# First feed-forward block by seven block products instead of eight, with its inner activations and the residual kept in DRAM

## What is computed

```python
x = x + y                                     # y = delta rule output @ w_out ("dn_out")
x = x + squared_relu_mlp(rms_norm(x, norm_mlp), mlp_w_up, mlp_w_down)
...
def squared_relu_mlp(h, w_up, w_down):        # 1024 -> 4096 -> 1024
    return jnp.square(jax.nn.relu(h @ w_up)) @ w_down
...
x = rms_norm(x, norm_final)                   # end of the first block
mx = split(silu(c) @ w_mod + b_mod, 6)        # modulation of the second block: needs no x
hx = rms_norm(x, g_norm1) * (1 + mx[1]) + mx[0]
```

## Time and profile before

| | |
|---|---|
| median of 3 runs | 3104.36 us (3101.61 to 3105.61) |
| profiled execution, its time | 3103.91 us |
| its span, first to last instruction | 3102.1 us |
| TensorE busy | 2953.6 us (95% of the span) |
| VectorE, ScalarE, GpSimd busy | 59%, 39%, 29% |
| mean granted TensorE clock | 0.987 |

### The profile page before, as it was taken

How to read it: one execution, slowest core, us unless ns; L and a number is a source line. 1 busy time by engine, 2 the same in 40 slices (tenths; PEclk the granted TensorE clock), 3 DMA queues, 4 the chain that set the end, 5 groups by cost and what they waited for, 6 DMA issues and landing times.

```text
span 3102.1 us, 37785 instructions
## 1 busy us (share of the span) xinstructions
PE 2953.6 (95%) x14715; PEld 2445.9 (79%) x14715; DVE 1820.8 (59%) x2359; ACT 1210.9 (39%) x1929; POOL 901.7 (29%) x684
## 2 busy tenths in 40 slices
PE   7899999989999999999998999999989999999997
PEld 6688888878788888888876777888878778887886
DVE  7566566564365544333366886554574866666866
ACT  5555555553311112221334776222332444444222
POOL 5333332221000000000302886331331444443423
PEclk9999999999999999999999999999999999999999
DMA  3111111112143333111210001011023144446953
GB/s 128 41 48 48 48 48 48 42 62 102 41 129 110 111 113 102 48 48 54 93 53 21 11 9 49 28 35 35 21 75 149 40 157 150 148 148 239 371 207 122
DMA packets 96833, 274.00 MB, mean 88 GB/s; under 512 B 9232, under 2 KB 31248, under 8 KB 92176
## 3 DMA queue, kind: packets, MB, share of 16 engines
q1 hardware_dynamic: 96656, 271.58, 25.0%
HBM read 208.43 MB, written 60.36 MB: 87 GB/s over the span
## 4 chain that ended last, share of the span: by engine, by line
PE 81%; DVE 10%; ACT 4%; issue 3%; POOL 1%; DMA 1%; SPq 0%; POOLq 0%; DVEq 0%; ACTq 0%
PE ps L663 25%; PE ps L1756 11%; PE ps L3068 11%; PE ps L3729 9%; PE ps L3096 7%; DVE b L3677 2%; PE ps L2659 2%; PE ps L1060 1%; DVE b L652 1%; PE ps L2466 1%; PE ps L2437 1%; PE ps L2465 1%; PE ps L1067 1%; PE ps L2480 1%; PE ps L90 1%
## 5 line engine op out<-in xcount | busy, mean ns | idle before, releaser
L663 PE MATMUL ps<-b 128*128 128x512 f32 x3912 | 1009.6, 403 | 29.7 <-DVE b L652 14.4
L663 PEld LDWEIGHTS ps<-b 128*128 128x128 f32 x3912 | 711.4, 191 | 159.2 <-issue 20.1
L1756 PE MATMUL ps<-b 128*128 128x512 f32 x1536 | 361.7, 396 | 0.6 <-DVE b L1924 0.6
L1756 PEld LDWEIGHTS ps<-b 128*128 128x128 f32 x1536 | 288.0, 188 | 69.5 <-DVE b L1924 1.0
L3729 PE MATMUL ps<-b 128*128 128x512 f32 (+1 forms) x1464 | 326.1, 377 | 6.3 <-ACT b L3788 5.9
L3729 PEld LDWEIGHTS ps<-b 128*128 128x128 f32 x1464 | 253.8, 191 | 55.6 <-issue 10.6
L644 ACT ACTIVATE b<-b 128x1024 fp32r<-128x1024 f32 x138 | 145.2, 1054 | 319.5 <-PE ps L1756 242.3
L3121 ACT ACTIVATE b<-b 128x512 fp32r<-128x512 f32 x232 | 142.3, 615 | 270.9 <-PE ps L3096 106.3
L652 DVE TENSOR_TENSOR b<-b 128x1024 fp32r<-128x1024 f32 x138 | 174.2, 1264 | 107.6 <-ACT b L644 98.5
L3068 PE MATMUL ps<-b 128*128 128x512 f32 x960 | 225.9, 393 | 6.0 <-DVE b L3371 3.8
L3068 PEld LDWEIGHTS ps<-b 128*128 128x128 f32 x960 | 180.5, 189 | 48.3 <-DVE b L3371 7.7
(11 more groups left out here) (372 smaller groups left out, 5011.4 us busy)
## 6 DMA issues: line engine op xcount, KB each, us to landing
inner<-b SPq DMA_DIRECT2D x77, 512.0 KB, 2.6
b<-inner SPq DMA_DIRECT2D x35, 1024.0 KB, 13.5
b<-in_down SPq DMA_DIRECT2D x52, 512.0 KB, 4.3
b<-in_mod SPq DMA_DIRECT2D x96, 256.0 KB, 2.6
b<-scratch SPq DMA_DIRECT2D x46, 512.0 KB, 4.4
b<-in_gu SPq DMA_DIRECT2D x44, 512.0 KB, 4.1
b<-in_dn_in SPq DMA_DIRECT2D x32, 512.0 KB, 4.9
b<-in_up SPq DMA_DIRECT2D x32, 512.0 KB, 3.7
```

What stands on the lines that cost most here:

```text
L663: ins = e.matmul(ps[:, c], w, h[:, k, c], start=first and k == 0 and i == 0, stop=last and k == KT - 1 and i == 2)
L1756: ins = e.matmul(ps[:, c], w, u[:, at[k], c], start=k == 0 and p == 0, stop=k == n - 1 and p == 2)
```

## The change

- The feed-forward block of the first layer goes by class `WideSquare`. The inner width of 4096 is 16 tiles v of 256. The first (v = 0) is computed plainly, by 96 matmuls; v = 1 to 15 and the 16 tiles of the down projection take 7 products of 12 matmuls each. A product is a step s, with (v, i) its tile and its number.
- In the up part every tile gives seven pieces (in the second layer it takes two tiles for seven), which go to a DRAM tensor and come back for the down part. x is stored to DRAM after the first residual sum, and read back in the down part; the output is summed in another tile, w.x.
- The norm's factor is not applied to the hidden activations but, squared, to the output: in the last tile (`dve_square_last`) VectorE multiplies each of 16 half rows of the output by it and then adds x, one waiting for the other.
- The modulation's generators are advanced in `pe_project`, twice per unit from the third on, and then at steps 6 to 94 that are multiples of 3, and later on even steps of the down part (`beside`).
- ScalarE starts the two squares per k of the second block's norm (`act_stat2`, now line 1612) when `x1` of k = 3 is complete, since the tiles that they are written to hold the output of k = 0 to 3 until then. GpSimd's 12 sums stay as they are.

Places in the order, and the generators' turns:

```diff
+BLOCKS1 = tuple(((2 * b, 2 * b + 1),) for b in range(8))
+PIECES7 = (0, 3, 5, 4, 1, 2, 6)
...
+    def piece(self, s):
+
+        n = self.na
+        for p in range(n):
+            if p < n - 2:
+                m = s - self.index[p, self.last(p)] - 2
+            else:
+                m, odd = divmod(s - self.index[n, 0] - 14 * (p - n + 2), 2)
+                m = -1 if odd else m
+            if 0 <= m < 7:
+                return p, m
+        return None
...
+    def sums(self, s):
+
+        if s == self.index[self.na, 0] + 13:
+            return self.na - 1
+        if s == self.index[0, 3] + 4:
+            return 0
+        v = self.which(s - 1, "last")
+        return v if v is not None and 0 < v < self.na - 1 else None
...
+    def beside(self, s):
+
+        a, b = self.index[self.na - 2, 0], self.index[self.na, 0]
+        return 6 <= s < a and s % 3 == 0 or s >= b and s % 2 == 0
...
+                if beside and k in (2, 5):
+                    next(beside)
```

SyncE's and TensorE's programs in the products:

```diff
+            piece = w.piece(s)
+            if piece:
+                p, n = piece
+                e.wait_ge(*V.at("tlo", p, n))
+                e.dma_start(self.scratch[4][PIECES7[n], :, p, :],
+                            w.stage[(7 * p + n) % 3].bitcast(F32)).then_inc(*self.hst[(7 * p + n) % 3].up(w.name, p, PIECES7[n]))
...
+            if (v, i) == (w.na + 6, 0):
+                for m in range(7 * w.na - 3, 7 * w.na):
+                    e.wait_ge(*self.hst[m % 3].at(w.name, m // 7, PIECES7[m % 7]))
+                for k in range(KT):
+                    e.wait_ge(*self.xl[k].at("x1_stored"))
+                    e.dma_start(self.x1[:, k, :], self.scratch[2][:, k, :]).then_inc(*self.xl[k].up("x1"))
...
+                if i == 2:
+                    e.wait_ge(*A.at("s1", v))
+                if i == 3:
+                    e.wait_ge(*A.at("s5", v))
+                if i == 4:
+                    e.wait_ge(*A.at("s2", v))
...
+                if i == 5 and v > 3:
+                    e.wait_ge(*V.at("q11", v - 2))
+                if i == 6:
+                    e.wait_ge(*V.at("q22", v))
```

ScalarE's:

```diff
+        for s in range(4, len(w.steps)):
+            v, i = w.steps[s]
+            t = v - w.na
+            if v < w.na:
+                u = w.quads(v)
+                if i in (0, 1, 2, 6):
+                    e.wait_ge(*P.at("st", v, i))
+                if i < 3:
...
+                    e.activation(u[name], self.square_bank(v, i % 2), ACT.Copy).then_inc(*A.up(("s1", "s5", "s2")[i], v))
+                if i == 6:
+                    if v >= 2:
+                        e.wait_ge(*V.at("tlo", v - 2, PIECES7.index(5)))
+                        e.wait_ge(*G.at("t", v - 2, 6))
+                    square(v, "21", self.square_bank(v, 0))
...
+            self.act_wide_high(e, w, s + 6)
+            if v < w.na and 3 <= i < 6:
+                name = ("12", "22", "11")[i - 3]
+                e.wait_ge(*V.at("q" + name, v))
+                square(v, name)
...
+                p, n = piece
+                m = 7 * p + n
+                product = PIECES7[n]
+                if m >= 3:
+                    e.wait_ge(*self.hst[m % 3].at(w.name, (m - 3) // 7, PIECES7[(m - 3) % 7]))
...
+                if product in (0, 3, 5):
+                    e.wait_ge(*A.at("sq", p, {0: "11", 3: "22", 5: "21"}[product]))
+                else:
+                    e.wait_ge(*G.at("t", p, product))
+                e.activation(w.stage[m % 3][:, 0:512], w.source(p, product), ACT.Copy).then_inc(*A.up("thi", p, n))
+            if v == last:
+                for k in {2: (0, 1), 3: (2, 3)}.get(i, ()):
+                    e.wait_ge(*V.at("x1", k))
+                    if k == 0:
+                        e.wait_ge(*V.at("x1", 3))
+                        e.wait_ge(*A.at("cw"))
+                    self.act_stat2(e, self.m1, w.sig, k)
...
+        for _ in beside:
+            pass
+        for k in range(4, KT):
+            e.wait_ge(*V.at("x1", k))
+            self.act_stat2(e, self.m1, w.sig, k)
+        self.act_weights(e, w.j0 + 2)
```

VectorE's:

```diff
+            if v < w.na:
+                if 3 <= i < 6:
+                    name = ("12", "22", "11")[i - 3]
+                    u = w.quads(v)[name]
+                    e.wait_ge(*P.at("st", v, i))
+                    if i == 3:
+                        e.wait_ge(*A.at("s2", v))
+                    e.tensor_tensor(u, u, self.square_bank(v, (1, 0, 2)[i - 3]), ALU.add).then_inc(*V.up("q" + name, v))
+            else:
+                self.dve_square_add(e, w, v - w.na, i)
+            self.dve_wide_low(e, w, s + 6)
+            piece = w.piece(s)
+            if piece:
+                p, n = piece
+                b = w.stage[(7 * p + n) % 3]
+                e.wait_ge(*A.at("thi", p, n))
+                e.tensor_tensor(b[:, 512:1024], w.source(p, PIECES7[n]), b[:, 0:512].bitcast(F32),
+                                ALU.subtract).then_inc(*V.up("tlo", p, n))
+            if v == last:
+                for k, f in {0: ((0, 0), (0, 1)), 1: ((1, 0), (1, 1)), 2: ((2, 0), (2, 1)), 3: ((3, 0), (3, 1), (4, 1), (6, 1)),
+                             4: ((5, 1), (7, 1)), 5: ((4, 0), (6, 0)), 6: ((5, 0), (7, 0))}[i]:
+                    self.dve_square_last(e, w, k, f)
...
+    def dve_square_last(self, e, w, k, f):
+
+        P, A, V, G = w.sig
+        c = HALVES[f]
+        y, x = w.x[:, k, c], self.x1[:, k, c]
+        e.wait_ge(*P.at("rw"))
+        e.wait_ge(*V.last())
+        e.tensor_tensor(y, y, self.psl[3][:, c], ALU.mult).then_inc(*V.up("scaled", k, f))
+        e.wait_ge(*self.xl[k].at("x1"))
+        e.wait_ge(*V.last())
+        ins = e.tensor_tensor(x, x, y, ALU.add)
+        ins.then_inc(*V.up("x1", k) if (f == 1) == (k < 4) else V.up("x1", k, "half"))
```

GpSimd's:

```diff
+            self.pool_wide_sums(e, w, s, 1)
+            p = w.sums(s)
+            if p is not None:
+                u, tq = w.quads(p), w.tq
+                if p:
+                    e.wait_ge(*V.at("tlo", p - 1, 6))
...
+                e.tensor_tensor(tq[0], u["12"], u["11"], ALU.subtract).then_inc(*G.up("t", p, 1))
+                e.wait_ge(*G.last())
+                e.tensor_tensor(u["12"], u["22"], u["12"], ALU.subtract).then_inc(*G.up("t", p, 4))
+                e.tensor_tensor(tq[1], u["22"], tq[0], ALU.subtract).then_inc(*G.up("t", p, 2))
+                e.wait_ge(*G.last())
+                e.tensor_tensor(tq[2], u["21"], tq[1], ALU.subtract).then_inc(*G.up("t", p, 6))
```

917 lines of the change are left out of this document (461 added, 456 removed).

## The result

The changed kernel takes 3163.7 us (median of 4 runs, 3162.3 to 3167.9), the kernel before 3103.8 us: ratio 1.0196, interval 1.0178 to 1.0213, 60 us slower. The forecast was 3107, the range up to 3134. The profiled execution's span is 3166.1 us, 64.0 more than before.

The account below looks back on a forecast made before the run. The prediction took TensorE's matmuls to bound the block. Its terms, -84.9 + 35 + 44 + 6 + 3 = +3 us on a span of 3102.1, gave a forecast of 3107 us, with an 8-in-10 range of 3072 to 3134.

Parts of the forecast that it names:

- What is removed, 84.9 us: First layer's feed-forward block: fewer product matmuls take TensorE from 706.7 to 621.8 us, -84.9 us.
- What is added at the end, +35: Last tile to next layer: GpSimd's sums start only after x1 of k = 3, +35 us with clock, bounds 25 and 40.
- What is added in the up part, +44: Twelve up-part rounds: a dependent chain of 21.5 us against TensorE's 20, plus pairs and clock, +44 us, bounds 5 and 70.
- By sums of busy time the others fit: Up-part round of 20.0 us on TensorE: ScalarE busy 15 us, GpSimd 10, VectorE 14, so each fits.
- the pairs: Up part: the modulation's VectorE instruction pairs delay the chain, 18 to 36 us over twelve rounds, taken as 22.
- the loop through the t sums: Up part: piece splitting, GpSimd's four t sums, S2 and q22 wait for each other in a 21.5 us chain per round.
- Smaller terms, entry +6: Block entry: late VectorE, waits for differences and squares, and two-column tiles, less old gap and clock: +6 us, bounds -4 and 16.
- Smaller terms, down part +3: Down part: 1 MB loads and stores as in the second layer, where TensorE stayed full: +3 us, bounds 0 and 8.
- Up-part traffic, 0: Up part: pieces, weights and modulation move about 290 GB/s, below the 379, so no cost.
- the chain is worse: Rival, 20%: up part, every pair meets GpSimd between q12 and q22, rounds of 25 us, up part 70, 3133 us.
- The full lock: Rival, 3%: VectorE and GpSimd exclude each other for whole instructions, 0.27 us more per meeting, 23 us in all, 3130 us.
- The marks named ahead: Signs: TensorE idle over 20 us at the end; up-part waits for 2009 and 3564; four t sums 6 us or more.

Follow-up runs that it names:

- e5: Changed kernel without the modulation's steps 3 to 9 of twelve (loads, VectorE instructions, small matmuls), so work is left out: 3123.4 us.
- e13: Changed kernel, with TensorE taking the modulation's small matmuls one pair later from its fifth step on and VectorE's accumulators alternating: 3162.2 us.
- e1: Changed kernel, with GpSimd's first three t sums waiting for earlier pieces and the fourth placed behind S2 and S4: 3159.7 us.
- e9: Changed kernel, with the four t sums of every tile made by VectorE instead of GpSimd: 3156.4 us.
- e6: Changed kernel without GpSimd's four t sums of tiles 1 to 15, so work is left out: 3129.6 us.
- e8: Changed kernel, with four buffers instead of two for the modulation's weights up to its tenth step: 3162.9 us.
- e14: Changed kernel, with the twelve operand differences at the block's entry made by VectorE instead of GpSimd: 3158.5 us.
- e7: Changed kernel, with the modulation's last six pairs and the context's work starting 20 steps later in the down part: 3153.2 us.
- e18: Changed kernel, with pieces of tiles 2 to 15 stored as 64 KB instead of 512, so work is left out: 3160.2 us.
- e10: Changed kernel, with up-part modulation pairs at products 0 and 5 of every tile and 6 of every second, not every third step: 3177.5 us.
- e2: Changed kernel, with VectorE's modulation instructions beside the up part cut to 4 of 512 columns, so work is left out: 3139.4 us.

## Why the prediction was wrong

- *What is removed, 84.9 us:* right. Undisturbed tiles take 19.1 to 19.4 us.
- *What is added at the end, +35:* right, +34.9, and by the steps given. GpSimd's 12 sums start 24.4 us after the last tile's start (23.1 foretold), take 30.5 and lie back to back. The next layer's first product comes at 64.9 us, 3 us later than the 62 foretold without the clock. The 3 us of clock did not come in that layer's products (96 in 22.06 us), but in part before them, where the granted clock was 0.54 up to 1612 us (windows above): the 32 small matmuls at 1608.72 took 5.86 us, the same count at full clock 3.74. One step was wrong without harm: the last tile's products end not after 19.2 us but after 30.5, because the last of them waits for VectorE's sums; GpSimd's chain ends later still.
- *What is added in the up part, +44:* the step that failed most in size, +67. Three of its terms are wrong. "By sums of busy time the others fit": VectorE was put at 14 us per round and is busy 19.6, because 5.4 instructions per round run beside GpSimd at 0.9 us extra each. I had the price of a meeting from the earlier trace rows and charged it to the t sums (0.8 us) and the pairs, not to the low parts of pieces and weights, the most frequent of VectorE's instructions and 38 of the 65 that were slowed. The check on it was misread too. In the 40 us of the third of the earlier trace rows I found 2 meetings from a busy time of 24.17 us, in which records that overlap count once; the 32 durations add up to 25.8 us, and five of them are 0.97 to 1.78. The second is the pairs: 22 us foretold, 40 measured (e5, waits and clock together). That TensorE itself stands for pairs, 11.8 us, was left out as well, but e13 took those waits away for nothing. The third is the clock: four long waits at 1 us each were foretold, and some 16 us came. The twelve rounds without pairs came to 22.3 us against my 21.5, which is luck: the loop through the t sums is not what sets them. e1 loosened it for 3 us, while moving the same sums away from VectorE's instructions gained 19 (e9) and leaving them out 36 (e6).
- *Smaller terms, entry +6:* 30.1 with the projection, outside its bounds. "VectorE enters the block some 4 us late" took VectorE's work in a unit as all there is, and the small matmuls that moved into the projection had no term. TensorE waits 6.3 us in the projection for a pair whose weights are late, has 5.7 us of small matmuls there that stood elsewhere before, and waits 5.8 and 6.8 us at the block's start. e8 and e14 each bring tile 2 forward by 4.7 us (projection included); the rest is not taken apart.
- *Smaller terms, down part +3:* +28, outside its bounds. The 1 MB loads themselves do no harm, as the earlier trace rows had it and e7's first three tiles show. What was overlooked is the modulation's 256 KB loads in the same queue, landing after 7.3 us in the median. e7 and e13 show that VectorE is what is late; e7 removed 12.8 us, and the rest came back two tiles further on, where the weights are late again.
- *Up-part traffic, 0:* right for the stores (e18).
- *Rivals:* "the chain is worse" had the size of what happened in the up part, rounds of 25 us, but not its mechanism: not pairs between q12 and q22 alone were slowed, and where e10 kept that place free of pairs, the rounds grew. Its 3133 us was too low, since it took the other terms from my own case. The full lock, by the Trainium skill (SBUF — State Buffer, section on who interferes with whom), was priced as 0.27 us on seven meetings. Its rule is borne out in kind by e2: an instruction of 0.22 us takes up to 1.26 beside a GpSimd instruction. A pair of full size alternates at 1.70 us, less than the 1.97 that the two durations add up to, so the lock's 0.27 us more per meeting did not show.

The marks named ahead are found: TensorE 22 us idle at the end, nine waits for 2009 of up to 7.2 us, rounds of 28.2, 30.0 and 28.9 us at every third tile from the sixth on, ScalarE waiting for 3564 (57.5 us) and four t sums of 6.4 us together. All of them fit the loop, and the loop was not the cause: VectorE being late leaves the same marks, and only e1 told the two apart. Rounds of 25.6 us and waits for 2138 were not among them.

Open are which of VectorE's late instructions ends which wait, why the place of the pairs costs 19 us in e10, and half of the down part's loss.

## What to carry to other kernels

A sum of busy times taken at an instruction's lonely duration is no proof that an engine fits: charge every two-input VectorE instruction that can stand beside GpSimd's with its measured duration there, and compare with the bound engine again. A mark that both explanations leave is no test of either; change the order of the waits, or move the work to another engine. Work that is spread "into idle time" needs its operands early as well. A small load beside 1 MB loads, with two buffers, made an in-order engine late here, and what stood behind it on that engine paid. And fewer matmuls raise the demand on every engine that feeds them: VectorE kept up at 12.2 us of a 19.3 us round and did not at 15.5, and only with both t sums and pairs left out, against a kernel that still does its modulation whole, did the 85 us leave 14 us.

## What the runs showed of the hardware

VectorE's and GpSimd's instructions with two SBUF inputs alternate when both have work: four and four took 6.87 and 6.85 us, 1.7 us each, against 0.69 and 1.29 alone. In e2 a VectorE instruction of four columns took 0.21 to 0.22 us in 43 places and 1.10 to 1.34 in 25, with nothing in between. VectorE's sums with one input in PSUM (2009) took 0.67 to 0.68 us in all 36 places of the twelve rounds, the 16 beside GpSimd included. ScalarE's durations (0.62 us in the median) did not change beside either.
